# Eight of eleven weight blocks of the down projection in half-width correction products in place of six, token sums in seven places

## What is computed

```python
proj = rmsnorm(h) @ w_in                     # q, f, v, g, u
o, S = hgrn2(q, f, v); pm = pool(u) @ w_pool
h = h + concat(o * silu(g), pm) @ w_out
gu = rmsnorm(h) @ w_gate_up                  # 2048 x 2*5632
h = h + (silu(gu[:, :D_FF]) * gu[:, D_FF:]) @ w_down      # 5632 x 2048, the part changed
e = rmsnorm(p @ w_ple)
h = h + sigmoid(h @ w_ple_gate) * e
y = rmsnorm(h)
```

## Time and profile before

| | |
|---|---|
| median of 3 runs | 1185.35 us (1182.74 to 1187.15) |
| the profiled execution | 1180.84 us, span 1178.8 us |
| mean granted TensorE clock | 0.995 |
| memory traffic | 226.89 MB read, 7.43 MB written, 199 GB/s over the span |
| loads of `w_down` | 88 of 512 KB, median 4.8 us from issue to landing |

### The profile page before, as it was taken

How to read it: one execution, slowest core, us unless ns; L and a number is a source line. 1 busy time by engine, 2 the same in 40 slices (tenths; PEclk the granted TensorE clock), 3 DMA queues, 4 the chain that set the end, 5 groups by cost and what they waited for, 6 DMA issues and landing times.

```text
span 1178.8 us, 30314 instructions
## 1 busy us (share of the span) xinstructions
PE 1163.9 (99%) x12182; PEld 1038.8 (88%) x12182; DVE 978.5 (83%) x1509; ACT 562.6 (48%) x804; POOL 55.5 (5%) x80
## 2 busy tenths in 40 slices
PE   9999999999999999999999999999999999999996
PEld 7888888888888899899998999999889999999885
DVE  6688599678867898998989989788897888887686
ACT  6445645555446744444434444444444444445442
POOL 2122210100000200000000000000000000000000
PEclk9999999999999999999999999999999999999998
DMA  7776775765566566666666666666666666667552
GB/s 257 242 231 178 233 213 180 226 181 189 175 219 197 179 213 198 201 193 201 205 212 196 195 199 195 213 208 196 196 209 189 206 205 198 196 197 249 166 158 74
DMA packets 193112, 234.89 MB, mean 199 GB/s; under 512 B 7987, under 2 KB 153626, under 8 KB 192761
## 3 DMA queue, kind: packets, MB, share of 16 engines
q1 hardware_dynamic: 187568, 220.29, 59.4%
q0 software_dynamic: 3968, 11.89, 3.5%
q10 hardware_dynamic: 1504, 1.70, 0.4%
HBM read 226.89 MB, written 7.43 MB: 199 GB/s over the span
## 4 chain that ended last, share of the span: by engine, by line
PE 90%; DVE 6%; ACT 2%; issue 1%; DMA 1%; ACTq 0%; SPq 0%; DVEq 0%
PE acc L2210 13%; PE acc L1816 10%; PE acc L1820 10%; PE acc L1818 10%; PE acc L2246 7%; PE acc L2212 6%; PE acc L2213 6%; PE acc L2191 5%; PE acc L2193 5%; PE wrk L2191 4%; PE wrk L2193 4%; PE acc L2248 4%; PE acc L2249 4%; DVE hl L952 2%; ACT hl L592 1%
## 5 line engine op out<-in xcount | busy, mean ns | idle before, releaser
L952 DVE SCALAR_TENSOR_TENSOR hl<-raw,hl 128x1024 f16<-128x1024 f32 x414 | 494.4, 1220 | 67.2 <-ACT hl L592 64.0
L592 ACT ACTIVATE hl<-raw 128x1024 f16<-128x1024 f32 x414 | 421.7, 1051 | 173.9 <-DMA raw<-in_w_down_dram 86.1
L2210 PE MATMUL acc<-nrm,hl 128*128 128x264 f16 x1344 | 274.8, 276 | 0.0
L1818 PE MATMUL acc<-nrm,hl 128*128 128x264 f16 x952 | 262.8, 276 | 0.0
L1820 PE MATMUL acc<-nrm,hl 128*128 128x264 f16 x952 | 262.7, 276 | 0.0
L1816 PE MATMUL acc<-nrm,hl 128*128 128x264 f16 x952 | 262.7, 276 | 0.0
L2212 PE MATMUL acc<-nrm,hl 128*128 128x264 f16 x672 | 185.5, 276 | 0.0
L2213 PE MATMUL acc<-nrm,hl 128*128 128x264 f16 x672 | 185.5, 276 | 0.0
L2246 PE MATMUL acc<-big,hl 128*128 128x264 f16 x704 | 146.2, 276 | 0.0
L2210 PEld LDWEIGHTS acc<-nrm,hl 128*128 128x128 f16 x1344 | 128.9, 98 | 17.8 <-DVE tg L1434 0.2
L1816 PEld LDWEIGHTS acc<-nrm,hl 128*128 128x128 f16 x952 | 93.3, 98 | 13.5 <-issue 0.4
(11 more groups left out here) (425 smaller groups left out, 2050.8 us busy)
## 6 DMA issues: line engine op xcount, KB each, us to landing
raw<-in_w_gate_up_dram SPq DMA_DIRECT2D x168, 512.0 KB, 4.6
raw<-in_w_down_dram SPq DMA_DIRECT2D x88, 512.0 KB, 4.8
raw<-in_w_in_dram SPq DMA_DIRECT2D x80, 512.0 KB, 4.4
raw<-in_w_out_dram SPq DMA_DIRECT2D x32, 512.0 KB, 4.8
raw<-in_w_ple_gate_dram SPq DMA_DIRECT2D x32, 512.0 KB, 5.2
state<-in_state_hgrn_dram POOLq DMA_DIRECT2D x8, 512.0 KB, 5.9
out_new_hgrn_sample_dram<-state POOLq DMA_DIRECT2D x8, 512.0 KB, 5.1
raw<-in_w_gate_up_dram SPq DMA_DIRECT2D x16, 256.0 KB, 3.3
```

What stands on the lines that cost most here:

```text
L592: nc.scalar.activation(hi[:, st.hl_slot(j, half), :], raw[:, st.raw_slot(j), :], ACT.Copy, scale=WSCALE).then_inc(hi_done, 1)
L952: stt(lo[:, st.hl_slot(j, half), :], raw[:, st.raw_slot(j), :], WSCALE, hi[:, st.hl_slot(j, half), :], ALU.mult, ALU.subtract).then_inc(lo ...
L1818: mm(out, wh, x_lo[:, kt, :], start=False, stop=False)
L2210: mm(out, wh, n_hi[:, kt, :], start=jj == 0 and kk == 0, stop=False, skip_group_check=bool(up))
```

## The change

Blocks 2 and 3 of groups 1 to 7 take the half-width form too: `DOWN_PAIRS` gets a fourth pair. That needs a fourth round of weight sums in each group and four more places of token sums, 16 in all. VectorE's sums of a pair are no longer spread between splits but made in a row: pair 0 ahead of split 4, pair 1 behind split 5, pair 2 behind split 7, pair 3 behind split 9. From pair 2 on they wait until TensorE has used the buffer. The token sums stand in seven pieces (8, 2, 2, 1, 1, 1, 1 places), the four new ones in memory of `s16`, `a32`, `tg32` and `gate_t`; two of the pieces (three places) are made at the end of the last FFN group, ahead of its combine, the other five in down group 0 where they were. The memset of h's sum of squares (it lies in `a32`) moves behind the last combine.

```diff
@@ -156,8 +156,10 @@
 HALF_T = TOK // 2
 FAST_PAIRS = (0, 1)
 NPAIRS = len(FAST_PAIRS)
-DOWN_PAIRS = (4, 6, 8)
-DOWN_T = ((0, 8), (8, 10), (10, 12))
+DOWN_PAIRS = (2, 4, 6, 8)
+DOWN_T = ((0, 8), (8, 10), (10, 12), (12, 13), (13, 14), (14, 15), (15, 16))
+T_SOON, T_LATE = (1, 3), (0, 2, 4, 5, 6)
+DOWN_SUMS = 3 * len(DOWN_PAIRS)
 IDLE_MMS = (37, 9, 2, 10, 6, 3)
 HALF_D = D // 2
 EARLY_SPLITS = (2, 4, 6, 8, 10, 12, 14)
@@ -310,8 +312,6 @@
         state = sb("state", [P, 2, NSAMP, P])
         s16 = sb("s16", [P, 2, NSAMP, P], F16)
         t16 = mix[:, :].bitcast(F16).rearrange("p (h f q t) -> p h f q t", h=2, f=4, t=HALF_T)
-        dt16 = [x.bitcast(F16).rearrange("p (h f q t) -> p h f q t", h=2, f=4, t=HALF_T)
-                for x in (mix[:, :], big[:, 2 * FFW:2 * FFW + 4 * TOK], spare[:, 660:660 + 4 * TOK])]
         s_hi = (s16[:, 0], xe[:, 512:1024].bitcast(F16).rearrange("p (b v) -> p b v", b=NSAMP))
         s_lo = (s16[:, 1], mix[:, 3584:4096].bitcast(F16).rearrange("p (b v) -> p b v", b=NSAMP))
         q16 = sb("q16", [P, HEADS, NSAMP, 2], F16)
@@ -322,6 +322,10 @@
         gate_t = sb("gate_t", [P, TPG, TOK])
         a32 = sb("a32", [P, 2, TOK])
         tg32 = sb("tg32", [P, 2, TOK])
+        dt16 = [x.bitcast(F16) for x in (mix[:, :], big[:, 2 * FFW:2 * FFW + 4 * TOK], spare[:, 660:660 + 4 * TOK])]
+        dt16 += [s16[:].rearrange("p a b v -> p (a b v)")[:, 0:4 * TOK]]
+        dt16 += [x.rearrange("p a t -> p (a t)").bitcast(F16) for x in (a32[:], tg32[:], gate_t[:, 0:2])]
+        dt16 = [x.rearrange("p (h f q t) -> p h f q t", h=2, f=4, t=HALF_T) for x in dt16]
         ident = sb("ident", [P, P])
         ones = sb("ones", [P, P])
         ident16 = sb("ident16", [P, P], F16)
@@ -1492,10 +1496,12 @@
                     dve.wait_ge(t_ready, 1 if f == 2 else 3)
                 token_sums(t16, n_both, f)
 
-            def token_sums_down(f, c):
-
+            def token_sums_down(f, cs, n):
+
+                c, m = cs[n], len(cs)
                 if f >= 2:
-                    dve.wait_ge(t_ready, 4 + c + (1 if f == 2 else 7))
+                    base = 4 + (0 if cs is T_SOON else 4 * len(T_SOON))
+                    dve.wait_ge(t_ready, base + (0 if f == 2 else 2 * m) + n + 1)
                 a, b = DOWN_T[c]
                 k0 = 4 * DOWN_PAIRS[0]
                 token_sums(dt16[c], ff_both[:, :, k0 + 2 * a:k0 + 2 * b, :], f)
@@ -1524,9 +1530,9 @@
                 j = DOWN_PAIRS[u]
                 if f == 0:
                     dve.wait_ge(lo_done, S_DOWN.block(i, j + 1) + 1)
-                    if u == 2:
+                    if u >= 2:
                         dve.wait_ge(used, S_DOWN.block(i, j - 3) + 1)
-                weight_sums(s_sum[(u + 1 - half) % 2], S_DOWN.hl_slot(j, half), f, down_sums, (i - 1) * 9 + 3 * u)
+                weight_sums(s_sum[u % 2], S_DOWN.hl_slot(j, half), f, down_sums, (i - 1) * DOWN_SUMS + 3 * u)
 
             def square_e(i):
 
@@ -1577,6 +1583,10 @@
                     split(nxt, i_nxt, j)
                     if between and j == 1:
                         between()
+                if nxt is S_DOWN:
+                    for f in range(4):
+                        for n in range(len(T_SOON)):
+                            token_sums_down(f, T_SOON, n)
                 up_ffn(i)
 
             with dve.Fori(0, KT - 1) as i:
@@ -1591,7 +1601,6 @@
                 wait_job("es")
                 rstd_row("es", 6).then_inc(e_rstd, 1)
                 dve.wait_ge(e_rstd, 1)
-                nc.vector.memset(h_ssq, 0.0)
 
             def next_low(i):
 
@@ -1622,10 +1631,12 @@
 
             def down_group(i, half, nxt, first=False):
 
-                def sums(u, f):
+                def sums(u):
                     if not first:
-                        down_sum(i, half, u, f)
-
+                        for f in range(3):
+                            down_sum(i, half, u, f)
+
+                sums(0)
                 split(S_DOWN, i, 4, half)
                 if first:
                     ff_low(S_FFN.groups)
@@ -1634,34 +1645,27 @@
                 split(S_DOWN, i, 5, half)
                 if first:
                     sum_of_e()
+                sums(1)
                 split(S_DOWN, i, 6, half)
-                sums(0, 0)
-                sums(0, 1)
                 split(S_DOWN, i, 7, half)
-                sums(0, 2)
-                sums(1, 0)
-                sums(1, 1)
+                sums(2)
                 split(S_DOWN, i, 8, half)
-                sums(1, 2)
                 split(S_DOWN, i, 9, half)
                 if first:
                     for f in range(2):
-                        for c in range(len(DOWN_T)):
-                            token_sums_down(f, c)
+                        for n in range(len(T_LATE)):
+                            token_sums_down(f, T_LATE, n)
+                sums(3)
                 split(S_DOWN, i, 10, half)
-                sums(2, 0)
-                sums(2, 1)
                 for j in range(AHEAD):
                     if nxt is S_DOWN:
                         split(S_DOWN, i + 1, j, 1 - half)
                     else:
                         split(nxt, 0, j)
-                    if j == 0:
-                        sums(2, 2)
-                        if first:
-                            for f in range(2, 4):
-                                for c in range(len(DOWN_T)):
-                                    token_sums_down(f, c)
+                    if j == 0 and first:
+                        for f in range(2, 4):
+                            for n in range(len(T_LATE)):
+                                token_sums_down(f, T_LATE, n)
                     if j == 1:
                         scale_e(i)
                 h = h_all[:, bass.ds(i * 2, 2), :]
@@ -1674,6 +1678,7 @@
                 dve.wait_ge(down_p1, i)
                 if nxt is not S_DOWN:
                     combine_last(last_banks, (i - 1) * 3)
+                    nc.vector.memset(h_ssq, 0.0)
                 else:
                     combine(banks[half], down_chain, (i - 1) * 3)
                 dve.wait_ge(acc_free, S_DOWN.tile(i, 2))
@@ -2167,8 +2172,6 @@
 
             def corrections(b, slot, s, q, x_hi, x_lo, kt, t, begin, end, done, n):
 
-                t, tq = t
-
                 def w(m, k):
                     return lambda h, a: hl[:, h, slot * BLOCK_KT * COLS + (2 * a + k) * 256 + m * P:][:, 0:P]
 
@@ -2179,7 +2182,7 @@
                     return lambda h, a: (x_hi, x_lo)[h][:, kt + 2 * a + k, c * HALF_T:(c + 1) * HALF_T]
 
                 def rs_(f):
-                    return lambda h, a: t[:, h, f, tq + a, :]
+                    return lambda h, a: t(h, f, a)
 
                 for out, left, right, ready in ((b.p2, w(0, 1), r(1, 0), 0), (b.p4, w(1, 1), rs_(3), 0),
                                                 (b.p1, w(0, 0), r(0, 0), 0), (b.p5, ws(0), rs_(0), 1),
@@ -2216,7 +2219,7 @@
                     if j == 4 + 2 * FAST_PAIRS[0]:
                         pe.wait_ge(t_ready, 4)
                     u = j // 2 - 2
-                    last = corrections(banks[1], slot, s_sum[u], 2 * (j % 2), n_hi, n_lo, 4 * jj, (t16, 2 * jj),
+                    last = corrections(banks[1], slot, s_sum[u], 2 * (j % 2), n_hi, n_lo, 4 * jj, lambda h, f, a: t16[:, h, f, 2 * jj + a, :],
                                        j == 4 + 2 * FAST_PAIRS[0], jj == 3,
                                        sum_ready, i * (3 * NPAIRS) + 3 * FAST_PAIRS.index(u))
                 last.then_inc(used, 1)
@@ -2227,6 +2230,11 @@
             out = job("es")
             pe.wait_ge(esum_ready, 2 * KT)
             mm(out[:, 0:TOK], ones[:], e_ssq, start=True, stop=True).then_inc(job_done, 1)
+
+            def t_piece(q):
+
+                c = [n for n, (lo_q, hi_q) in enumerate(DOWN_T) if lo_q <= q < hi_q][0]
+                return dt16[c][:, :, :, q - DOWN_T[c][0], :]
 
             def down_block(i, half, j, plain, final=False):
 
@@ -2254,10 +2262,9 @@
                         pe.wait_ge(t_ready, 4 + 4 * len(DOWN_T))
                     u = j // 2 - DOWN_PAIRS[0] // 2
                     q = 2 * (j - DOWN_PAIRS[0])
-                    c = [n for n, (lo_q, hi_q) in enumerate(DOWN_T) if lo_q <= q < hi_q][0]
-                    last = corrections(b, slot, s_sum[(u + 1 - half) % 2], 2 * (j % 2), ff_hi, ff_lo, 4 * j,
-                                       (dt16[c], q - DOWN_T[c][0]), j == DOWN_PAIRS[0], j == DOWN_PAIRS[-1] + 1,
-                                       down_sums, (i - 1) * 9 + 3 * u)
+                    last = corrections(b, slot, s_sum[u % 2], 2 * (j % 2), ff_hi, ff_lo, 4 * j,
+                                       lambda h, f, a: t_piece(q + a)[:, h, f], j == DOWN_PAIRS[0], j == DOWN_PAIRS[-1] + 1,
+                                       down_sums, (i - 1) * DOWN_SUMS + 3 * u)
                 last.then_inc(used, 1)
 
             def down_group(i, half, plain=False, final=False):
```

## The result

The change makes the kernel slower: 1195.3 us (median; 1194.5 to 1197.1) against 1182.7 for the kernel before, run beside it (1181.3 to 1187.2); the ratio is 1.0102, with a 95% interval of 1.0085 to 1.0119. The prediction was 1202 us, with 0.83 on slower by over 0.5%. The profiled execution took 1194.51 us, its span is 1192.7 (before 1180.84 and 1178.8), and its mean granted clock 0.993.

A forecast was written before the change was run, and what follows sets the result against it. TensorE bounded the kernel; VectorE's loop through split 10 and loads would take over: 22.3 + 9.0 - 0.1 = 31.3 us per group, seven periods, +17.4 us on the median 1185.35, so 1202 us, range 1186 to 1212.

The forecast's parts named there:

- The products: Down groups on TensorE: half-width blocks take 2.51 us against 2.70 plain, so a group takes 28.18, 0.38 less.
- VectorE's list: VectorE's steps in a down group, from the combine's first add: block 10 is split 22.3 us later, before 16.5.
- C: Start of the combine's first add on VectorE in a down group, from which the prediction counts times.
- the first C: Group 1's combine start, put on the same count: 873.9, after token sums that lose nothing at the beginning.
- The waits: VectorE waits about 4 us a group before splits 2 and 3, none before the combine; TensorE waits for VectorE.
- X: Time from the end of split 10 to the end of the next group's split 3: 9.0 us, between 6.6 and 10.7.
- the forecast's band: Split 10 to the next group's split 3 takes 8.2 to 10.7 us, time 1197 to 1214; chance 0.70.
- rival 2: The same down-group loop, milder: split 10 to next split 3 takes 6.7 to 8.1 us, time 1187 to 1197; chance 0.12.
- group 0's three loads: Nearest row for loads behind split 10: three issued in a burst from 865.17, split 3 ended at 874.03, giving 9.0 us.
- rival 1: TensorE stays the down stage's bound, period at most 28.3 us, time 1182.7 at best; chance 0.14.
- The clock: Rival: TensorE's stops in down groups lower the granted clock too, time about 1215 us; chance 0.04.
- Rival 4: The change doesn't do what it says and the added pairs' blocks stay plain; chance under 0.01.

The follow-up runs named there:

- the spread versions: Changed kernel with weight sums spread between splits: 1184.30 us; also block 10 in slot 3: 1182.70; also the gate stage's block 2 not waiting for split 10: 1180.65.
- The run with the token sums alone: Changed kernel's token sums with the three pairs and weight-sum order of the kernel before: 1181.87 us, ratio 0.9998 to the kernel before.
- the other slot for block 10: Changed kernel with block 10 of a down group landing in slot 3, so the next group's block 2 need not wait for split 10: 1191.15 us.
- the runs with short loads: Changed kernel with loads of blocks 2 and 3, or of blocks 0 to 3, of every down group cut to 128 KB: 1189.63 and 1187.92 us.
- four short loads: Changed kernel with loads of blocks 0 to 3 of every down group cut to a quarter of their bytes: 1187.92 us, ratio 1.0038.
- less work: Changed kernel without pair 3's weight sums on VectorE, TensorE taking those of pair 1 instead (partly wrong result): 1188.33 us, ratio 1.0049.
- two short loads: Changed kernel with loads of blocks 2 and 3 of every down group cut to 128 KB: 1189.63 us, ratio 1.0050.

## Why the prediction was right, and where it was off

**The products.** Right. Between waits, half-width blocks still follow each other in 2.51 us (942.57 to 945.08), and a group where nothing is late takes 28.18 us, to the hundredth (the spread versions). The 81 ns that the Trainium skill gives as the sustained gap (TensorE: Matmul & The Clock Gate, Back-to-back issue gap) would have made the change a loss on TensorE alone; the rows differ, with 57.5 ns for 132 columns.

**VectorE's list.** Right: split 10 at C + 22.3 was predicted, and C + 22.2 to 22.3 measured (in group 1, counted from the update of h, 20.5). One reading was wrong without a consequence: behind split 10 of before stood not two thirds of a pair's sums but all of them, and the 2.5 us are the price of all.

**The token sums and the first C.** Right. A sum over 264 elements has a pace of 0.20 to 0.21 (0.20 estimated). On the prediction's count the first C is 877.45 + 0.85 - 2.66 = 875.6 (0.85 from the start of the update of h to the next instruction), less the 1.9 by which this execution's down stage began later: 873.8, predicted 873.9. That this is so near is in part luck. I had the last FFN group's combine 0.9 us late and VectorE through with block 3 at 875.7. The combine still waited 0.61 us for ScalarE, VectorE was through at 876.62, so at 874.8 on that count, and then waited 0.82 us for TensorE, which set the start. The run with the token sums alone fits: no cost in its time.

**The waits.** Right in kind: VectorE's wait ahead of the combine vanished, TensorE waits at the corrections and at the gate stage, ScalarE for the loads. Not in size: I expected the waits ahead of blocks 2 and 3 to be some 4 us per group. They are 0.8 to 1.2 (0.67 + 0.32 in the rows above), and 2.2 and 2.4 in the two long groups, with another 1.0 to 1.3 ahead of block 1 (in the last group ahead of block 0), of which I had said nothing.

**X, the mis-sized term.** From the end of split 10 to the end of split 3 I took 9.0 us, out of bounds of 6.6 and 10.7. (The terms of the lower one add up to 6.7.) Measured, over the seven groups: 7.6, 8.9, 9.0, 7.6, 7.6, 7.6, 7.9, a mean of 8.0. Seven times 1.0 is 7 us, and it is the whole miss of the down stage: +17.4 predicted, +10.4 measured. By the prediction's own cases this is not the forecast's band (8.2 to 10.7) but the upper edge of its rival 2, the milder loop (chance 0.12), 1187 to 1197 us; the median is inside the stated range because the range took that rival in. The choice that failed was to take group 0's three loads as the nearest row. There block 2 needed 5.2 us from issue to ScalarE; in the new order four groups of seven look like this (after, SyncE's issue of block 2's load, and ScalarE's starts):

```profile
1020.32 0.37 SPq L463 DMA_DIRECT2D raw<-in_w_down_dram  x1
```

```profile
1018.86 1.06 ACT L596 ACTIVATE hl<-raw 128x1024 f16<-128x1024 f32 x1 [4.08 <-DMA raw<-in_w_down_dram]
1021.52 1.06 ACT L596 ACTIVATE hl<-raw 128x1024 f16<-128x1024 f32 x1 [1.61 <-DMA raw<-in_w_down_dram]
1023.98 1.06 ACT L596 ACTIVATE hl<-raw 128x1024 f16<-128x1024 f32 x1 [1.40 <-DMA raw<-in_w_down_dram]
```

Block 2 is issued at 1020.32 and with ScalarE at 1023.98: 3.7 us, all but the 3.6 of a load with little beside it. The text had said it (blocks 0 and 1 are ahead by 5 and 4 us "and nearly landed"), and then it took the row in which they were not. What speaks for this cause: the landing grows with how close the loads stand (3.5, 5.9 and 6.8 us in one burst, with the other slot for block 10). What stays open: in two of the seven groups the same order gave 4.9 us (issued at 928.25, with ScalarE at 933.18) and 5.1, and X of 8.9 and 9.0. The trace sets these two apart in one thing: a transfer of 16 KB of instructions (the queue of kind "instruction") begins while block 2's load is under way, and in the other five groups none does. The queues from block 2's issue to its landing in the first long group, and then in the group behind the second one, where the landing took 3.6 us:

```profile
q1 hardware_dynamic: 1278, 1.27, 78.3%
q8 instruction: 1, 0.02, 2.1%
```

```profile
q1 hardware_dynamic: 841, 0.84, 70.9%
```

In the runs with short loads it is the same two groups, with landings of 3.1 to 3.8 us in place of 2.3. That such a transfer delays the load is not shown: no run was made for it, and in before block 2's landings with one (5.1 to 6.7 us) are no longer than without (5.9 to 6.8). The Trainium skill (DMA: Bandwidth & Descriptors, Latency and other measured facts) says that a lighter load on HBM goes with a smaller fixed cost. The 3.7 against 5.2 us agree in direction. I named the rule and let it lean towards rival 1 only, and didn't let it move X.

**The clock.** I gave it a rival with 0.04 and 30 us, and left it out of the sum. Inside the groups it does fall once (0.62 between 973 and 976 us and 0.81 between 976 and 979, behind a wait of 1.34) and costs nothing that shows: TensorE waits for VectorE there anyway. It was missed at the one place where TensorE is the bound right behind a stop, the gate stage: 1.7 us. "Nothing after it gives this back" was right, but something after it added.

**The sum.** The predicted difference in span was 17.4; measured 1.9 + 10.4 + 1.7, together 13.9 before rounding. The 7 us too much in X were partly made up by the clock's 1.7 and by the 1.9 of an execution that began the stage late; so the size is nearer than its parts. In the medians, +12.6 against my +16.7. The other 2.7 of the 6.7 us between 1202 and 1195.3 are no mechanism: I built on a median of 1185.35 us, and the kernel before, measured beside the change, has 1182.7.

**The rivals.** Rival 1 (TensorE stays the bound) needed X up to 6.1. No group had it. With four short loads, groups with 6.0 and 5.9 have periods of 28.2 and 28.1, so its condition was right, and not met. Rival 4 is out, as TensorE's blocks show the new form.

## What to carry to other kernels

When an engine has slack, ask what the order of its work does for the others: here VectorE's splits free the slots from which loads go out, and the sums stood between them as spacers, which kept the loads apart. Packing work together on one engine makes bursts on the next: four loads issued within 2.8 us took until 9.4 us after the first issue to be usable. Work whose place is free belongs behind the release that others wait for, where it fills the wait. Read the loop (release, load, split, combine) and not the sum of work; and at the end of a stage, ask for each saving whether the last group, whose end is the handover, should have it.

## What the runs showed of the hardware that was not expected

- **A load's time falls little with its size.** 128 KB took 2.4 to 3.9 us from issue to use in three groups of the same kernel, 512 KB with little beside it 3.6. What else is under way matters more: 6.8 us for the third of three 512 KB loads issued within 1.7 us.
- **GpSimd and VectorE slow each other, and which of the two loses changes from group to group.** Beside a GpSimd product of two tensors, each of the eleven float16 subtractions that it overlapped took 1.23 us in place of 0.68. A float32 split beside one took 1.73 to 1.80 us in four cases and its usual 1.22 in five. In three of the four slow cases GpSimd's own product took 0.74 to 0.82 us; beside the splits that kept their time it took 1.78 or more. The Trainium skill (SBUF — State Buffer, Who interferes with whom) says that a VectorE instruction with two SBUF inputs contends with a GpSimd instruction that reads SBUF. The subtractions agree, and so do the splits.
- **A stop of 3.3 us on TensorE was followed by half the clock for about 3 us**, 1.7 us of time; products without use in the stop kept it at full speed. In two other runs (less work, two short loads) stops of 3.2 and 3.6 us were followed by some 6 us of it and a rest 2.7 and 2.9 us longer.
